# A two-block transformer forward pass: the input's second half is loaded later, the first weight unit is used row by row, and TensorE gets three products of zeros at the start

## What is computed

```python
h = rmsnorm(x, norm_attn_g)          # x: 256 x 1024
u = h @ w_in                         # w_in: 1024 x 5632, in columns: q, k, v, pool, gates
q, k, v, u_pool, u_gate = split(u)
# then differential attention, pooling, gates, w_out, an MLP (w_up, w_down),
# and a second block with sparse attention, gated linear attention,
# cross attention and a convolutional MLP; a last rmsnorm
```

## Time and profile before

| | us |
|---|---|
| runs shown, median (lowest to highest of 3) | 811.46 (811.17 to 812.76) |
| the profiled execution's own time | 811.38 |
| its span, first to last instruction | 809.3 |
| PE busy | 796.4 |
| DVE busy | 601.4 |
| ACT busy | 471.0 |

### The profile page before, as it was taken

One profiled execution on the slowest core, in us unless ns is written; L12 is line 12 of the kernel. 1 busy time (PEld: TensorE's weight loads), 2 busy tenths in 40 slices (PEclk: granted clock), 3 DMA queues, 4 the chain that ended last, 5 costly groups with the idle time before them and its releaser, 6 DMA issues.

```text
span 809.3 us, 11468 instructions
## 1 busy us (share of the span) xinstructions
PE 796.4 (98%) x4517; PEld 678.4 (84%) x4517; DVE 601.4 (74%) x1004; ACT 471.0 (58%) x837; POOL 28.6 (4%) x52
## 2 busy tenths in 40 slices
PE   7999999999999999999999999999999999999997
PEld 6878888888888888889999778888888888888885
DVE  6788776978777864558569787777678898999644
ACT  6666555646555644446377565763487776667443
POOL 4100000000000000000310000000000000000000
PEclk9999999999999999999999999999999999999999
DMA  9854644455755655544866434265543555555541
GB/s 329 243 166 152 197 154 156 156 182 163 254 179 186 207 172 193 198 164 144 251 192 205 157 109 153 105 156 181 169 145 111 200 170 197 193 175 205 189 174 53
DMA packets 81638, 143.38 MB, mean 177 GB/s; under 512 B 5122, under 2 KB 35872, under 8 KB 81584
## 3 DMA queue, kind: packets, MB, share of 16 engines
q1 hardware_dynamic: 78976, 136.72, 51.6%
q0 software_dynamic: 2160, 5.46, 2.3%
q10 hardware_dynamic: 448, 0.47, 0.2%
HBM read 141.05 MB, written 1.05 MB: 176 GB/s over the span
## 4 chain that ended last, share of the span: by engine, by line
PE 96%; DVE 2%; DMA 1%; ACT 0%; issue 0%; SPq 0%; DVEq 0%
PE PS L1333 93%; PE PS L1348 4%; DMA X<-in_x_dram 1%; DVE low_r L2519 0%; ACT HT_r L1980 0%; ACT WK_f L1977 0%; DVE WK_f L2523 0%; DVE AR_f L2519 0%; SPq L3471 0%; DVE AR_f L2523 0%; DVE st L3214 0%; DVE WK_f L2519 0%; DVE HT_f L2519 0%; DVE st L2792 0%; DVE HT_r L2519 0%
## 5 line engine op out<-in xcount | busy, mean ns | idle before, releaser
L2519 DVE TENSOR_TENSOR low_r<-low_f,high 128x1024 fp32r<-128x1024 f32 (+1 forms) x256 | 299.6, 1204 | 72.1 <-ACT high L1980 71.5
L1980 ACT ACTIVATE high<-low_f 128x1024 fp32r<-128x1024 f32 (+1 forms) x264 | 257.5, 1024 | 93.7 <-DMA low_f<-in_w_down_dram 39.7
L1333 PE MATMUL PS<-high,AR_r 128*128 128x512 f32 (+2 forms) x724 | 215.0, 377 | 0.0
L1333 PE MATMUL PS<-HT_r,high 128*128 128x512 f32 (+2 forms) x896 | 209.8, 356 | 0.0
L1333 PE MATMUL PS<-high,HT_r 128*128 128x512 f32 (+1 forms) x576 | 187.9, 395 | 0.3 <-ACT HT_r L1980 0.3
L1333 PEld LDWEIGHTS PS<-HT_r,high 128*128 128x128 f32 (+1 forms) x896 | 150.9, 188 | 17.0
L1333 PEld LDWEIGHTS PS<-high,AR_r 128*128 128x128 f32 (+1 forms) x724 | 129.2, 181 | 25.9 <-issue 0.7
L1333 PE MATMUL PS<-low_r,AR_r 128*128 128x512 f32 (+2 forms) x362 | 133.9, 374 | 0.0
L1333 PEld LDWEIGHTS PS<-high,HT_r 128*128 128x128 f32 x576 | 107.8, 189 | 23.9 <-issue 2.1
L1333 PE MATMUL PS<-HT_r,low_r 128*128 128x256 f32 (+1 forms) x712 | 121.9, 282 | 0.3 <-DVE low_r L2519 0.3
L1333 PEld LDWEIGHTS PS<-HT_r,low_r 128*128 128x128 f32 (+1 forms) x712 | 107.4, 189 | 9.0 <-DVE low_r L2519 0.5
(11 more groups left out here) (176 smaller groups left out, 699.8 us busy)
## 6 DMA issues: line engine op xcount, KB each, us to landing
low_f<-in_w_in_dram SPq DMA_DIRECT2D x39, 1024.0 KB, 5.2
low_f<-in_w_up_dram SPq DMA_DIRECT2D x38, 1024.0 KB, 5.2
low_f<-in_w_down_dram SPq DMA_DIRECT2D x27, 1024.0 KB, 4.9
low_f<-in_w_out_dram SPq DMA_DIRECT2D x8, 1024.0 KB, 5.0
low_f<-in_w_xkv_dram SPq DMA_DIRECT2D x4, 1024.0 KB, 5.5
low_f<-in_w_branch_gla_dram SPq DMA_DIRECT2D x2, 1024.0 KB, 5.0
low_f<-in_w_branch_nsa_dram SPq DMA_DIRECT2D x4, 512.0 KB, 5.9
low_f<-in_w_xq_dram SPq DMA_DIRECT2D x2, 1024.0 KB, 5.3
```

The source lines that it names most:

```text
L1333: return nc.tensor.matmul(o, l, r, start=start, stop=stop, skip_group_check=True)
L1980: return nc.scalar.activation(o, i, ACT.Copy, bias=0.0, scale=1.0)
L2519: return nc.vector.tensor_tensor(o, a, b, op)
```

## The change

SP's list: the two row tiles of the input's first half stay first; then come all four rows of the first weight unit; the two row tiles of the second half follow behind it. The first unit is used row by row, row 0 for i = 0 and i = 1, then row 1 for both, and so on (8 steps of 3 fast products). The half-1 turns stand in the list behind the first half of that unit (rows 0 and 1, 12 fast products), and ScalarE's and VectorE's steps around them are in a new order. `self.rings["big"] += 2` moves the ring on, so that k gets banks 0 and 1 (q now has 2 and 3). VectorE clears 384 columns of AR before anything else, and TensorE multiplies those zeros three times (128x128 by 128x256, fp32) into bank 7, which nothing reads, ahead of its first step.

```diff
@@ def wide
-                    for q in range(2):
-                        self.step("wide", key=key, j=j, u=u, k0=k0, i=q, use=uses[q], last=last,
-                                  ks=range(2 * i, 2 * i + 2))
+                    for k in range(2 * i, 2 * i + 2):
+                        for q in range(2):
+                            self.step("wide", key=key, j=j, u=u, k0=k0, i=q, use=uses[q], last=last, ks=range(k, k + 1))
@@ class Schedule
-    def first_turns(self):
-
-        for i in range(2):
-            self.turn_ht(0, i, 0, "X", self.big)
-            if i == 0:
-                self.step("quarter_hi", k=0)
-        for k in range(1, 4):
+    def first_turns(self, first):
+
+        self.turn_ht(0, 0, 0, "X", self.big)
+        self.step("quarter_hi", k=0)
+        self.turn_ht(0, 1, 0, "X", self.big)
+        self.turn_lo(0, 0, 0)
+        self.step("quarter_hi", k=1)
+        self.step("quarter_lo", k=0)
+        self.turn_lo(0, 1, 0)
+        self.step("quarter_lo", k=1)
+        for k in range(2, 4):
             self.step("quarter_hi", k=k)
-        for i in range(2):
-            self.step("quarter_lo", k=i)
-            self.turn_lo(0, i, 0)
+        self.n_split = self.n_low = 3
+        next(first)
         for i in range(2):
             self.step("quarter_lo", k=2 + i)
+        self.step("split_hi", u=1, parts=(0,))
+        for i in range(2):
             self.turn_ht(0, i, 1, "X", self.big)
-            if i == 0:
-                self.step("split_hi", u=1, parts=(0,))
+        self.rings["big"] += 2
+        next(first)
+        self.turn_lo(0, 0, 1)
         self.step("split_hi", u=1, parts=(1,))
-        for i in range(2):
-            self.turn_lo(0, i, 1)
-            self.step("split_lo", u=1, parts=(i,))
+        self.step("split_lo", u=1, parts=(0,))
+        self.turn_lo(0, 1, 1)
+        self.step("split_lo", u=1, parts=(1,))
         for i in range(2):
             self.step("first_squares", i=i)
         for i in range(2):
             self.step("first_roots", i=i)
         self.n_split = self.n_low = 2
+        self.ahead(3)
+        self.lows()
@@ def run
-        self.first_turns()
-
         first = self.wide("q", 0, evac=True, pairs=True)
-        next(first)
+        self.first_turns(first)
         self.step("angles")
@@ tensor_program
+            pe.wait_ge(s_zeros, 1)
+            for _ in range(3):
+                mm(PS[:, 7, 0:256], AR[:, 0:128], AR[:, 128:384], True, True)
@@ vector_program
+            nc.vector.memset(AR[:, 0:384], 0.0).then_inc(s_zeros, 1)
             nc.vector.memset(eps[:, 0:1], 1.0).then_inc(s_eps, 1)
@@ sync_program
+            for i in range(2):
+                nc.sync.dma_start(X[:, i, 0:512], xd[:, i, 0:512]).then_inc(s_x[i][0], 16)
             for j in range(2):
-                for i in range(2):
-                    h = slice(512 * j, 512 * j + 512)
-                    nc.sync.dma_start(X[:, i, h], xd[:, i, h]).then_inc(s_x[i][j], 16)
                 nc.sync.dma_start(w0[:, j], first[:, j]).then_inc(s_w0[j], 16)
             nc.sync.dma_start(w0[:, 2:4], first[:, 2:4]).then_inc(loaded[0], 16)
+            for i in range(2):
+                nc.sync.dma_start(X[:, i, 512:1024], xd[:, i, 512:1024]).then_inc(s_x[i][1], 16)
```

More of the change, by code:

```diff
@@ L1206, in two_blocks @@
         s_w1 = sem("load_second")
-        s_qh, s_ql = sem("quarter_hi"), sem("quarter_lo")
+        s_qh, s_ql, s_zeros = sem("quarter_hi"), sem("quarter_lo"), sem("zeros")
         s_id, s_g0, s_cst, s_vr, s_pos, s_lam = (sem("load_" + n) for n in ("id", "g0", "cst", "vr", "pos", "lam"))
```

## The result

| | before | changed |
|---|---|---|
| median of 16 runs each, us | 811.60 | 813.36 |
| lowest to highest | 811.10 to 812.76 | 812.61 to 814.53 |
| profiled execution, its time | 811.38 | 812.61 |
| its span | 809.3 | 810.6 |

The ratio is 1.0023, with a 95% interval of 1.0016 to 1.0029: slower. The forecast was 811.3, no change, with a range up to 813.3; the median lies 0.06 outside it. The profiled execution is the fastest of the sixteen, so the trace shows less than the usual loss (four of the sixteen took 814.16 to 814.53, eleven 812.96 to 813.55).

What follows compares the result with a forecast made beforehand. TensorE's and ScalarE's chains were taken to meet at 26.5 us; TensorE's 0.84 lead shrank by waits of 0.28 and 0.39, ScalarE gave 26.45 for 26.53, so 811.38 became 811.3; range 810.4 to 813.3.

Steps and rivals of the forecast that it cites:

- I take full speed from there: TensorE from about 5.5 us, in the middle of the half-0 turns: its clock stays at the upper level from then on.
- The clock: TensorE's start: busy from 1.35 to 6.4 us with at most 0.4 of break, its clock rises near 5.5 after 4.15.
- The rival: Gap before the first product loses the zeros' effect: 0.20 us per slow product, ten give 813.3; nine or more, chance 0.14.
- the same -0.08: Transposes of q start at 26.45 instead of 26.53 us, the forecast's whole gain.
- The two chains that meet at 26.5: At q's transposes TensorE's chain and ScalarE's, from the last `turn_ht`, meet with nothing between; both must come forward to gain.
- The forecast case: Full-speed products from the first at 8.4 us, transposes of q at 26.45, time 811.3; chance 0.56.
- The two waits for VectorE: TensorE waits for `low_r` of the second unit near 14.7 and 16.4 us, losing 0.28 and 0.39.
- The transfers: Input DMA: rows 2 and 3 land near 8.35 us, input's second half near 9.0 and 9.65, second unit about 11.0; costs nothing.
- Zeros: Three products of zeros start near 1.35 us and end at 3.95 to 4.3, before the gains land; cost nothing.
- The change does nothing: Rival: zeros leave the clock as it is, six products slow; +1.1 us, 812.5, inside the middle case of chance 0.12.

Runs made afterwards that it cites:

- early_squares: Changed kernel with ScalarE's sums of squares of row tile 0 moved into its idle time and the norm's roots behind the split of unit 2: 813.03 us, ratio 1.0021.
- before_filled: Kernel before plus three products of zeros at the start and one more behind each pair of turns: 811.43 us, ratio 0.9997.
- Filled_gap: Changed kernel with four more products of zeros on TensorE behind the half-0 turns: 811.70 us, ratio 1.0001 to the kernel before.
- changed_again: The changed kernel, nothing altered, run once more to see another execution: 814.24 us, one run.
- before_zeros: Kernel before with only the memset and three products of zeros at the start: 811.32 us, ratio 0.9994.
- filled_half: Changed kernel with two more products of zeros behind the half-0 turns: 811.73 us, ratio 1.0000 to the kernel before.
- early_turns: Changed kernel, four filler products, squares of tile 0 early, roots and last `turn_lo` later, half-1 turns after six products instead of twelve: 810.89 us, ratio 0.9989.

## Why the prediction was wrong

**The step that failed** is "I take full speed from there", under "The clock". I priced the rise by 4.15 us of unbroken work and then let it last over an idle stretch that the same sum had shown: 1.9 to 2.4 us before the first product. Both halves failed. The level fell in that gap in the execution profiled (granted clock 0.50 from about 7.7), and in another it had never risen (5.1 us of zeros and transposes, transposes still 1.97). The sum set down nothing for either, where the runs show 0.20 us for each of seven to twelve products. Filling the gap took 1.66 us off the median (813.36 to 811.70, with 811.60 and 811.48 of the kernel before beside them), and this is nearly all of the change's loss.

**The rival was the right one, at a chance of 0.14.** Its mechanism, the place (the moved turns) and its price hold: 0.20 per product, measured as 0.204. Its "ten products, 813.3" stands beside a median of 813.36, in part by luck: the count at the median is in no trace, and the rival's sum starts from the same -0.08 as the forecast, which was 0.35 too low (see below). I gave it 0.14 because "5.1 us of work where 4.15 sufficed" seemed strong. But 4.15 was one execution; the same work ahead gave seven products at the lower level in one run and twelve in another. A single trace says that a level was reached, not when it is reached in the others.

**The two chains that meet at 26.5 were right.** The changed kernel's squares and transposes of q moved by 1.19 and 1.16; with ScalarE's part taken off, TensorE alone held the end (early_squares); with the clock kept in the old order, ScalarE did (before_filled). There the kernel before's slow products had cost little, 0.2 by the traces.

**The forecast case itself was mis-sized by 0.35.** Filled_gap is what I described: products at full speed from the first. Foreseen 26.45 for the transposes of q, measured 26.80. The first product started at 8.54, not 8.40 (0.14: VectorE's step ended 0.04 later than summed, at 8.39, and TensorE started 0.15 behind it, where I had allowed 0.05); the third gain step at 12.03, not 11.73; the squares at 14.84, not 14.52. The two waits for VectorE were there, one ahead of 15.39 and one near 16.9.

**The transfers were right.** Rows 2 and 3 of the unit were used from 8.37 (foreseen 8.35), the second unit from 11.09 (11.0), and the input's second half was never waited for. Zeros: 1.32 to 4.25, as foreseen.

**"The change does nothing"**, with 812.5 for six products, comes close to the profiled execution (812.61) by luck. There the zeros had raised the clock for the half-0 turns, seven products were slow, and they started 0.45 earlier than in filled_gap.

## What to carry to other kernels

Warming TensorE up pays only if no long idle stretch stands between the warm-up and the work (2.43 us lost the level here, 0.76 did not) and if TensorE is what the next stage waits for. Place the filler right ahead of the first real product, and check the pace of the products, not the profile's clock column alone. When work is moved behind the first products, price the hole that it leaves as well as what it delays, and see which engine's chain begins with it. A clock's rise read from one execution is one draw: look at several before building a sum on it.

## What the runs showed of the hardware that I had not expected

- The clock column reads 1.00 until the first change that is recorded: in the changed kernel's second trace (changed_again) it is 1.00 from 4 to 13 us, while the products came 0.43 apart. Where it showed a fall, it had first risen.
- The level can fall after two idle stretches of 0.48 and 1.04 us with 1.3 us of transposes between them (before_zeros), and can stay up over 0.76 (filled_half) and 0.70 (early_turns).
- Products of zeros can raise it too, in some executions and not in others. Behind the same 2.93 us of them, the eight half-0 transposes took 1.09 in two of ten traces, 1.16 to 1.83 in four, and 1.97, as without zeros, in four.
- The unbroken work before it rose differs as much: 3.0 us of products in the changed kernel's first trace (8.09 to about 11.1), 5.3 in its second (8.59 to 13.85), 4.15 of transposes and products in the kernel before.
